# A two-block transformer forward pass: one of four weight halves per chunk of the state stage is split by GpSimd instead of VectorE

## The reference, cut to what matters

```
u, z = split(h @ w_in, 2)                       # w_in is 2048 x 4096
bu   = per group of 16 channels: B (64 x 16, complex) times u
x_t  = a * x_(t-1) + bu_t                       # complex, 64 states in each of 128 groups
y    = gelu(Re(C x) + d_skip * u)
out  = (y * sigmoid(y @ w_glu + b_glu) * silu(z)) @ w_out
```

## Time and profile before

| | |
|---|---|
| median of 3 runs | 3165.0 us (3164.55 to 3169.92) |
| profiled execution, its own time | 3174.17 us |
| its span in the profile | 3172.4 us |
| PE busy, share of the span | 98% |
| DVE, ACT, POOL busy | 70%, 47%, 4% |
| granted TensorE clock, mean | 0.99 |
| state stage in the span | from about 1985 to about 2260 us |

### The profile page before, as it was taken

One profiled execution on the slowest core, in us unless ns is written; L12 is line 12 of the kernel. 1 busy time (PEld: TensorE's weight loads), 2 busy tenths in 40 slices (PEclk: granted clock), 3 DMA queues, 4 the chain that ended last, 5 costly groups with the idle time before them and its releaser, 6 DMA issues.

```text
span 3172.4 us, 52938 instructions
## 1 busy us (share of the span) xinstructions
PE 3095.9 (98%) x19348; PEld 2705.8 (85%) x19348; DVE 2231.7 (70%) x2987; ACT 1502.7 (47%) x2065; POOL 128.3 (4%) x146
## 2 busy tenths in 40 slices
PE   7999999999999998999999999899999999999998
PEld 7888888888888888999889997888888788888887
DVE  5778887667767657766666655999865657566665
ACT  6455444554343444343443344656544534455553
POOL 0000000000000000000000000444100000000000
PEclk9999999999999999999999999899999999999999
DMA  6676776558877765777877765344455478644445
GB/s 239 214 249 241 255 277 210 170 185 282 280 250 278 279 220 196 275 260 254 292 242 272 258 238 183 107 137 141 137 179 173 158 240 299 221 153 153 153 146 186
DMA packets 191458, 688.61 MB, mean 217 GB/s; under 512 B 21904, under 2 KB 26256, under 8 KB 189968
## 3 DMA queue, kind: packets, MB, share of 16 engines
q1 hardware_dynamic: 183744, 669.07, 61.4%
q10 hardware_dynamic: 7504, 16.56, 1.5%
HBM read 683.45 MB, written 2.10 MB: 216 GB/s over the span
## 4 chain that ended last, share of the span: by engine, by line
PE 79%; DVE 10%; ACT 2%; issue 1%; DMA 1%; ACTq 0%; DVEq 0%; SPq 0%
PE psum L769 43%; PE psum L752 16%; PE psum L733 9%; PE psum L735 4%; DVE ring_parts L2191 2%; DVE work L2376 2%; PE psum L783 1%; DVE arena_high L2382 1%; PE psum L854 1%; DVE arena_high L2381 1%; PE psum L796 1%; PE psum L974 1%; DVE work L2338 1%; DVE work L2339 1%; DMA ring<-in_stream 1%
## 5 line engine op out<-in xcount | busy, mean ns | idle before, releaser
L2191 DVE TENSOR_TENSOR ring_parts<-ring,hi_parts 128x1024 fp32r<-128x1024 f32 x1002 | 1201.4, 1231 | 356.2 <-ACT hi_parts L1296 350.4
L1296 ACT ACTIVATE hi_parts<-ring 128x1024 fp32r<-128x1024 f32 x1002 | 1025.1, 1057 | 642.8 <-DMA ring<-in_stream 607.4
L752 PE MATMUL psum<-arena_low_parts,hi_parts 128*128 128x256 f32 x4000 | 744.6, 285 | 5.5 <-DVE arena_low_parts L1911 3.6
L769 PE MATMUL psum<-hi_parts,arena_high_parts 128*128 128x512 f32 x2224 | 731.1, 394 | 0.0
L769 PE MATMUL psum<-hi_parts,arena_low_parts 128*128 128x512 f32 x2064 | 672.0, 392 | 0.1
L752 PEld LDWEIGHTS psum<-arena_low_parts,hi_parts 128*128 128x128 f32 x4000 | 631.6, 193 | 18.1 <-issue 8.5
L752 PE MATMUL psum<-arena_low_parts,ring_parts 128*128 128x256 f32 x2064 | 586.1, 284 | 0.0
L769 PEld LDWEIGHTS psum<-hi_parts,arena_high_parts 128*128 128x128 f32 x2224 | 417.9, 188 | 90.2 <-issue 3.5
L769 PE MATMUL psum<-ring_parts,arena_low_parts 128*128 128x512 f32 x1184 | 461.4, 390 | 0.0
L769 PEld LDWEIGHTS psum<-hi_parts,arena_low_parts 128*128 128x128 f32 x2064 | 387.9, 188 | 80.9 <-issue 0.8
L752 PEld LDWEIGHTS psum<-arena_low_parts,ring_parts 128*128 128x128 f32 x2064 | 398.3, 193 | 0.0
(11 more groups left out here) (370 smaller groups left out, 2455.1 us busy)
## 6 DMA issues: line engine op xcount, KB each, us to landing
ring<-in_stream SPq DMA_DIRECT2D x1272, 512.0 KB, 4.3
arena_high<-in_mem ACTq DMA_DIRECT2D x2, 1024.0 KB, 5.9
arena_high<-in_x ACTq DMA_DIRECT2D x1, 2048.0 KB, 12.2
arena_low<-in_x ACTq DMA_DIRECT2D x1, 2048.0 KB, 9.3
arena_high<-in_ssm_bc ACTq DMA_DIRECT2D x64, 32.0 KB, 2.3
arena_high<-in_ssm_bc ACTq DMA_DIRECT2D x16, 128.0 KB, 3.3
out<-arena_low SPq DMA_DIRECT2D x4, 512.0 KB, 4.1
arena_high<-in_decay ACTq DMA_DIRECT2D x1, 1024.0 KB, 4.6
```

The source lines that it names most:

```text
L752: mm = pe.matmul(bank[:, half:half + S], r32(w[:, slot, cols]), r32(x[part][:, k, :]), start=(k == 0 and n == 0), stop=(k == KT - 1 and n ...
L769: mm = pe.matmul(stream_bank(b + t), r32(x[part][:, kg * KG + kk, t * P:(t + 1) * P]), r32(w[:, slot, cols]), start=(kg == 0 and kk == 0 a ...
L1296: act.activation(r32(hi[:, g % RING, cols]), ring[:, g % RING, cols], ACT.Copy).then_inc(hi_made, 1)
L2191: dve.tensor_tensor(r32(slot), slot, as32(hi[:, g % RING, cols]), ALU.subtract).then_inc(cut_done, 1)
```

## The change

DVE no longer cuts the second half of su(cc+2) between its two groups of scans. POOL does it, after `turned(cc+1)`, with the same subtraction. It waits for ACT's upper half (`hi_made`) and signals its own semaphore `pool_cut`. PE waits for `pool_cut` before it uses such a half. DVE's next cut, the first half of the unit behind it, raises `cut_done` by 2 in place of 1, so that the count of later halves and SP's waits stay as they were. There are 15 such halves.

```diff
+POOLED = {POS[("unit", "su", _u)] + LEAD: _u - 1 for _u in range(1, D // P)}
...
-        cut_done = sem("cut_done")
+        cut_done, pool_cut = sem("cut_done"), sem("pool_cut")
...
             def cut_half(phase, u, h, i=None, per=0):
 
                 g = POS[("unit", phase, u)]
+                if h == 1 and g in POOLED:
+                    pe.wait_ge(pool_cut, POOLED[g] + 1)
+                    return g % RING
...
-                        dve.tensor_tensor(r32(slot), slot, as32(hi[:, g % RING, cols]), ALU.subtract).then_inc(cut_done, 1)
+                        dve.tensor_tensor(r32(slot), slot, as32(hi[:, g % RING, cols]),
+                                          ALU.subtract).then_inc(cut_done, 2 if h == 0 and g - 1 in POOLED else 1)
...
                 scans(cc, 0)
-                if later:
-                    cut(POS[("unit", "su", cc + 1)] + LEAD, halves_=(1,))
                 scans(cc, 1)
...
+            def cut_second_half(g):
+
+                cols = slice(HALF, 2 * HALF)
+                slot = ring[:, g % RING, cols]
+                pool.wait_ge(hi_made, 2 * HI[g])
+                pool.tensor_tensor(r32(slot), slot, as32(hi[:, g % RING, cols]), ALU.subtract).then_inc(pool_cut, 1)
...
                 if cc + 1 < SSM_CHUNKS:
                     turned(cc + 1)
+                    cut_second_half(POS[("unit", "su", cc + 1)] + LEAD)
```

## The result

The changed kernel takes 3184.3 us in the median of 6 runs (3182.2 to 3186.9), against 3164.6 us for the kernel before (6 runs, 3161.3 to 3169.9). The ratio is 1.0066, with a 95% interval of 1.0056 to 1.0077: slower by 19.7 us. I had forecast no change, in a range up to 3179. The profiled execution of the changed kernel took 3186.6 us, and its span 3184.8 us.

The account below looks back on a forecast made before the run. Two regimes in the state stage: DVE bounds early chunks (17.65 us), PE late ones (16.34). 13 x 16.9 against 222.9 us gives -3.2, odd chunks +3, about 0: 3165 us, range 3155 to 3179.

Parts of the forecast that it names:

- Its price to DVE: State stage: POOL's 1024-element cut delays DVE 2.0 us where it collides, bounds 0 and 2.4.
- The new wait: PE's wait for POOL's half, used behind outputs: POOL done over 12 us ahead, so cost 0.
- The sum: State stage total: -3.2 us over 13 chunks plus 3 for two odd chunks, about 0.
- Two odd chunks: First chunk and gelu chunk: ACT is late, POOL's cut misses DVE's free time; 3 us together.
- The baseline of 222.9 us for 13 chunks: Kernel before, state stage: 141.2 us for eight early chunks plus 81.7 for five late ones.
- early eight gain 6: First eight timed chunks, 17.65 us each before, gain 6 us; the late five lose 2.8.
- The settled loop, 16.9 us: DVE's loop per settled chunk after the change: 13.42 us uncontended plus contention from POOL, 16.9 us.
- free stretch: DVE's time in products, skip and direct_block, T + 1.0 to T + 4.0 (T: inputs' end), where POOL's cut costs about nothing.
- 13.42 + 1.35 + 0.86 + 0.4 + 0.4 + 0.43: Settled loop: DVE uncontended, turned, one 128x512, two 128x256 sums, about half the other 128x512.
- The check of the early regime: Early chunks before the change: 14.55 + 1.35 + 1.71, both 128x512 on sz cuts, 17.61 against 17.65 us measured.
- POOL's cut takes the port while DVE needs it: Rival: POOL's cut between sz cuts costs DVE 2.0 to 2.4, both 128x512 0.86 each; 3176 us, chance 0.30.
- threshold of 17.1 us: DVE loop length, 222.9 / 13, above which the port rival was to decide.

Follow-up runs that it names:

- e2_no_cut: Changed kernel with POOL's subtraction replaced by a signalling nop and PE multiplying the upper half instead of the lower, waits kept: 3161.6 us, ratio 0.9993.
- second and third profile: Kernel before, unedited, profiled twice more; profiled executions took 3165.9 and 3167.5 us, with 16.34 us per chunk from chunk 2 on.
- e5_gate_cut: Changed kernel with POOL's cut also held back until DVE has ended both sz cuts: 3182.6 us, ratio 1.0041.
- three places tried: POOL's cut in the changed kernel, held back until after the sz cuts, or moved behind ssm_w in POOL's queue: 17.30, 17.35 and 17.32 us per chunk.
- e8_half_of_it: Changed kernel with POOL cutting only 512 columns of the half and DVE the other 512, PE waiting for both: 3176.1 us, ratio 1.0031.

## Why the prediction was wrong

- **The length of POOL's instruction, 2.4 us:** right, 2400 ns in the median.
- **Its price to DVE, 2.0 us where it collides, 0 to 2.4:** right in kind, 2.19 us measured up to the start of the products. By the exclusive lock of a whole instruction that I cited from the Trainium skill's "SBUF — State Buffer", section "SBUF: two separate sides", it would be 2.4; the measurement lies between.
- **The new wait costs 0:** right. In e2_no_cut all waits are there and the time is 0.9993 of before.
- **The products of DVE feel nothing:** right, 0.68 us beside POOL's pair in both kernels.

The sum was -0.2 us, and the two spans differ by 20.7. Three steps of it failed. By size:

- **Two odd chunks, 3 us together above 16.9 each: 9.2 short, the largest part.** Chunk 1 takes 25.49 us and the gelu chunk 20.52, together 46.0 where the sum has 36.8. Chunk 1 of the kernel before takes 19.73 and 21.81 us in the second and third profile; the first had it at 17.08, the shortest of all.
- **The baseline of 222.9 us for 13 chunks: 7.1 too high.** I summed it from one profiled execution, and then took the 9 us by which this execution was slower than the median as an offset that stands outside the stage. In the second profile the same 13 chunks take 19.73 + 12 x 16.34 = 215.8 us, and 217.9 in the third. My "early eight gain 6" had nothing to gain from. With 215.8 the rest of my sum gives 219.7 + 3 - 215.8 = +6.9 us: slower, by a third of what was measured.
- **The end of the stage, put at nothing without a reason: 4.7 us.** The last period takes 16.32 us instead of 15.37, and the tail behind it 3.8 more, most of it DVE's lateness.

9.2 + 7.1 + 4.7 - 0.2 = 20.8 us, against the 20.7. In the mechanism, what failed is the place at which I let POOL's cut run:

- **The settled loop, 16.9 us: too short by 0.4.** I put POOL's cut in the free stretch, and said that DVE's lateness would slide a 128x512 into it. DVE had that state in three chunks (17.05, 17.02 and 17.09 us); each time the lateness went on until the cut itself stood between the two sz cuts. In the terms of the sum, 13.42 + 1.35 + 0.86 + 0.4 + 0.4 + 0.43, the last four terms were to be 2.1 us; with turned at 1.3 and fractions at 0.4, the cut costs 2.19, and 13.42 + 1.3 + 0.4 + 2.19 = 17.3. Even with the cut held in the free stretch (e5_gate_cut) the loop is 17.35, so the sum was mis-sized there too. That PE's eleven ordinary chunks nevertheless take 16.90 us in the mean is luck: four of them take PE's own 16.3 to 16.4 us, on a lead that DVE had from elsewhere, and the lateness is paid in the tail.
- **The check of the early regime, 17.61 against 17.65 us, agreed by luck.** The 17.61 takes both of POOL's products to fall on the sz cuts in each chunk. They did so in three of eight; in the other five one fell there, and in three of these the other fell on back. DVE's loops were 16.7 to 18.6 us, and the 17.65 is PE's mean with the gelu chunk of 19.92 in it.
- **The rival that came true** is the second one, "POOL's cut takes the port while DVE needs it", at its named place, between the sz cuts. Its two 128x512 did not pay, since they lie beside the products. Its threshold of 17.1 us was taken from the same wrong baseline. The real one is 16.34, PE's work: any contention of more than 2.92 us in a loop costs, and what was measured is 17.30 - 13.42 = 3.88.

**The place mattered little, the balance did.** A chunk offers POOL about 3 us beside DVE's products, skip and direct_block (2116.94 to 2119.93). In the kernel before, ssm_w's pair (2.67 us) fills it. Another 2.4 us of reading by POOL, in each of the three places tried, pushed something of about equal length onto DVE's other instructions, and 1.1 us came back. That three places gave the same chunk within 0.05 us, and half of the work 0.37 us over PE's 16.34 instead of 0.96, is the evidence. What the time would be with the whole of POOL's reading inside DVE's PSUM stretches was not tried; this kernel has no room of that size.

## What to carry to other kernels

Before you sum a stage from one profiled execution, compare that execution's own time with the median; if they differ by more than the effect that you look for, find out in which stage, for it may be the one you cost. Work handed from VectorE to GpSimd is not free for VectorE: a two-input subtraction cost it nearly the whole time of GpSimd's instruction (2.19 of 2.39 us), unless it fell beside VectorE's reads of PSUM. So ask how much of that cover is still free, and not only whether GpSimd is idle. And ask first what a free removal would bring: here leaving the cut out altogether gained nothing measurable.

## What the runs showed of the hardware that I had not expected

- POOL can get its turn between two instructions of DVE that stand back to back. POOL got in between two sz cuts 1.07 us after the first had begun (the first cut alone takes 1.13), and the pair became 2.19 us longer; in e8_half_of_it POOL came just behind the start of a cut and waited 1.14 us itself. A POOL duration can hold waiting: the 512-column cut reports 2.37 us there, about what 1024 columns take.
- A GpSimd memset of 128x1024 (0.95 us) left VectorE's two-input rotations at 0.41 us, a cut at 1.22 and a pair of cuts at 2.35. Each was seen once.
- A long pause of PE was paid twice here. Behind 6.54 us of standing still outputs take 1.94 instead of 1.08 us, at a granted clock of 0.50, the lower of TensorE's two levels (1.2 GHz). At the end of the stage a pause of 3.35 us at a granted clock of 1.00 is followed by three groups of outputs, the last of which takes 1.92 us where it took 1.07 in the kernel before; the granted clock over them is 0.58.
- The same program ran this stage in two ways, with 16.7 to 19.9 us or with 16.34 us per chunk over chunks 2 to 8. In the former, one or both of POOL's products fell on the sz cuts (3.20 or 4.06 us instead of 2.35). One of three profiles showed it. What sets it off stays open.
